# Differential attention: the two probability maps combined by ScalarE and GpSimd instead of one VectorE pass

## What is computed

```python
def _diff_scores(q, k, v, lam):
    """q (B,Q,H,2,d), k (B,K,H,2,d), v (B,K,H,2d) -> (B,Q,H,2d)."""
    s = jnp.einsum('bqhmd,bkhmd->bhmqk', q, k).astype(F32) * DIFF_SCALE
    p = jax.nn.softmax(s, axis=-1)
    attn = p[:, :, 0] - lam * p[:, :, 1]
    return jnp.einsum('bhqk,bkhe->bqhe', attn.astype(v.dtype), v)
```

## Time and profile before

| | before |
|---|---|
| median of 3 runs | 4101.81 us (4099.81 to 4107.31) |
| the profiled execution | 4105.7 us, span 4103.9 us |
| mean granted TensorE clock | 0.935 of full speed |
| PE busy | 3507.0 us (85%) |
| PE weight loads | 2879.6 us (70%) |
| DVE busy | 2514.7 us (61%) |
| ACT busy | 1064.3 us (26%) |
| POOL busy | 779.5 us (19%) |

### The profile page before, as it was taken

One profiled execution on the slowest core, in us unless ns is written; L12 is line 12 of the kernel. 1 busy time (PEld: TensorE's weight loads), 2 busy tenths in 40 slices (PEclk: granted clock), 3 DMA queues, 4 the chain that ended last, 5 costly groups with the idle time before them and its releaser, 6 DMA issues. The chain is left out here.

```text
span 4103.9 us, 51032 instructions
## 1 busy us (share of the span) xinstructions
PE 3507.0 (85%) x19424; PEld 2879.6 (70%) x19424; DVE 2514.7 (61%) x5060; ACT 1064.3 (26%) x1823; POOL 779.5 (19%) x464
## 2 busy tenths in 40 slices
PE   6798999999687775996997878999998788859888
PEld 2687888888577774775783666788886677737577
DVE  4136577753289995765554234677763799967554
ACT  2112222222144443332111211222211444413310
POOL 3233333332100001110002233433332000012000
PEclk8899999999899997998998989999999899989999
DMA  5253222232343312334325154232232633123432
GB/s 203 57 153 126 91 90 94 90 99 73 106 127 92 91 34 94 106 99 164 106 82 190 50 136 151 77 94 92 89 99 67 173 85 85 38 103 112 133 115 70
DMA packets 414142, 424.54 MB, mean 103 GB/s; under 512 B 56940, under 2 KB 350572, under 8 KB 412742
## 3 DMA queue, kind: packets, MB, share of 16 engines
q1 hardware_dynamic: 368876, 319.55, 27.0%
q10 hardware_dynamic: 45024, 101.73, 7.0%
HBM read 288.28 MB, written 124.53 MB: 101 GB/s over the span
## 5 line engine op out<-in xcount | busy, mean ns | idle before, releaser
L734 PE MATMUL l_p_acc<-l_u_hi,l_p_w_hi 128*128 128x512 f32 (+1 forms) x2240 | 612.7, 376 | 47.8 <-POOL l_p_w_lo L649 37.2
L734 PE MATMUL l_p_acc<-l_u_hi,l_p_w_lo 128*128 128x512 f32 (+1 forms) x2240 | 593.2, 367 | 0.0
L734 PE MATMUL l_p_acc<-l_u_lo,l_p_w_hi 128*128 128x512 f32 (+1 forms) x2240 | 592.3, 367 | 0.0
L734 PEld LDWEIGHTS l_p_acc<-l_u_hi,l_p_w_hi 128*128 128x128 f32 x2240 | 390.9, 190 | 126.5 <-POOL l_p_w_lo L649 37.8
L734 PEld LDWEIGHTS l_p_acc<-l_u_hi,l_p_w_lo 128*128 128x128 f32 x2240 | 386.0, 189 | 72.2
L734 PEld LDWEIGHTS l_p_acc<-l_u_lo,l_p_w_hi 128*128 128x128 f32 x2240 | 385.9, 189 | 72.2
L647 POOL TENSOR_TENSOR l_p_w_hi<-l_p_wt,l_p_zero 128x1024 fp32r<-128x1024 f32 x104 | 209.9, 2019 | 974.2 <-PE l_p_acc L734 807.7
L2014 POOL TENSOR_TENSOR l_sd_xend<-l_sd_tok,l_sd_mine 128x512 f32<-128x512 f32 x80 | 85.5, 1071 | 1285.9 <-ACT l_sd_tok L1969 1285.1
L1471 PE MATMUL l_at_pS<-l_at_k_hi,l_at_q 128*128 128x512 f32 (+1 forms) x400 | 166.3, 416 | 148.6 <-ACT l_at_prob L1586 114.0
L649 POOL TENSOR_TENSOR l_p_w_lo<-l_p_wt,l_p_w_hi 128x1024 fp32r<-128x1024 f32 x104 | 272.7, 2622 | 8.2
L1655 DVE TENSOR_REDUCE l_at_nmax<-l_at_pS 128x1 f32<-128x1280 f32 (+1 forms) x144 | 197.1, 1369 | 84.4 <-PE l_at_pS L1472 81.3
(11 more groups left out here) (329 smaller groups left out, 7067.8 us busy)
## 6 DMA issues: line engine op xcount, KB each, us to landing
l_p_wt<-w_in SPq DMA_DIRECT2D x104, 512.0 KB, 3.9
l_n_wa<-w_ada SPq DMA_DIRECT2D x10, 2048.0 KB, 18.4
xbc_d<-l_p_fin ACTq DMA_DIRECT2D x32, 640.0 KB, 2.9
kf_d<-l_p_R SPq DMA_DIRECT2D x72, 256.0 KB, 3.5
l_o_oT<-o_d SPq DMA_DIRECT2D x18, 1024.0 KB, 6.7
l_at_K<-kf_d SPq DMA_DIRECT2D x64, 256.0 KB, 2.9
l_o_rows<-w_out SPq DMA_DIRECT2D x32, 512.0 KB, 4.5
qk_d<-l_p_late ACTq DMA_DIRECT2D x12, 1280.0 KB, 4.8
```

The lines of the kernel that those rows point to most:

```text
L734: mm = pe.matmul(acc[:, a:a + w], (w_hi, w_lo)[wp][:, m % 2, k], (u_hi, u_lo)[up][:, k, t0 + c:t0 + c + w], start=(k == n == 0), stop=(k = ...
```

## The change

DVE's `combine` becomes `factor`: the reciprocal and the factor stay, the pass over the keys goes. ACT gets `scale_map(i-1)`, which multiplies the second map by the factor in place; it stands behind `copy(i-2, 1)` and ahead of `exp(i, 0)`. POOL gets a program of its own with one `tensor_tensor` add per unit, which writes `mix` and increments `mixed`. Two semaphores are new: `back_ready` (DVE to ACT) and `map_scaled` (ACT to POOL). Buffers and all other code are the same.

```diff
+                def scale_map(n):
+                    h, q = units[n]
+                    act.wait_ge(back_ready, n + 1)
+                    second = prob[:, (2 * n + 1) % 3, 0:keys(q)]
+                    act.activation(second, second, ACT.Copy, scale=back[:, n % 2:n % 2 + 1]).then_inc(map_scaled, 1)
+
...
                     if turning > 2:
                         copy(i - 2, 1)
+                    if 1 <= i < NU + 1:
+                        scale_map(i - 1)
                     if i < NU:
                         exp(i, 0)
...
+            @block.gpsimd
+            def _(pool):
+                for n, (h, q) in enumerate(units):
+                    pool.wait_ge(map_scaled, n + 1)
+                    if n >= 2:
+                        pool.wait_ge(turned, before[n - 1])
+                    w = keys(q)
+                    pool.tensor_tensor(mix[:, n % 2, 0:w], prob[:, 2 * n % 3, 0:w], prob[:, (2 * n + 1) % 3, 0:w], ALU.add).then_inc(mixed, 1)
...
-                def combine(n):
+                def factor(n):
                     h, q = units[n]
                     s = n % 2
                     dve.wait_ge(exped, 2 * n + 2)
                     dve.reciprocal(recip[:, n % 4], sums[:, s]).then_inc(mix_step, 1)
-                    dve.wait_ge(mix_step, 2 * n + 1)
-                    dve.tensor_scalar(back[:, s:s + 1], recip[:, n % 4, 1:2], sums[:, s, 0:1], lam[:, 0:1], ALU.mult, ALU.mult).then_inc(mix_step, 1)
-                    dve.wait_ge(mix_step, 2 * n + 2)
-                    if n >= 2:
-                        dve.wait_ge(turned, before[n - 1])
-                    dve.scalar_tensor_tensor(mix[:, s, 0:keys(q)], prob[:, (2 * n + 1) % 3, 0:keys(q)], back[:, s:s + 1], prob[:, 2 * n % 3, 0:keys(q)], ALU.mult, ALU.add).then_inc(mixed, 1)
+                    dve.wait_ge(mix_step, n + 1)
+                    dve.tensor_scalar(back[:, s:s + 1], recip[:, n % 4, 1:2], sums[:, s, 0:1], lam[:, 0:1], ALU.mult, ALU.mult).then_inc(back_ready, 1)
```

More of the change, by code:

```diff
@@ L1334, in attention_hyena_stage @@
     with stage(nc, tag + "lam_in", tag + "s00_in", tag + "s01_in", tag + "s10_in", tag + "s11_in", tag + "v0_in", tag + "v1_in",
-               tag + "lam_step", tag + "lam_exp", tag + "scored", tag + "maxed", tag + "exped", tag + "mix_step", tag + "mixed", tag + "turned",
+               tag + "lam_step", tag + "lam_exp", tag + "scored", tag + "maxed", tag + "exped", tag + "mix_step", tag + "back_ready", tag + "map_scaled", tag + "mixed", tag + "turned",
                tag + "turned_copied", tag + "pv_done", tag + "squared", tag + "log_done", tag + "rms_ready", tag + "scaled", tag + "o_turned",
@@ L1340, in attention_hyena_stage @@
                tag + "q_mm", tag + "q_copied", tag + "z_step", tag + "out_ready", tag + "hy_stored") as (ctx, sems):
[L1341 to L1344, removed]
+        (lam_in, s00_in, s01_in, s10_in, s11_in, v0_in, v1_in, lam_step, lam_exp, scored, maxed, exped, mix_step, back_ready, map_scaled, mixed, turned, turned_copied,
+         pv_done, squared, log_done, rms_ready, scaled, o_turned, gated, stored0, stored1) = sems[:27]
+        u_in, x_in, k_in = sems[27:31], sems[31:35], sems[35:37]
+        (kn_in, mats_in, rows_turned, rows_copied, dft_step, r_ready, x_mm, prod_step, y_ready, q_mm, q_copied, z_step, out_ready, hy_stored) = sems[37:]
         stored = (stored0, stored1)
@@ L1738, in _ @@
                     if 1 <= i < NU + 1:
-                        combine(i - 1)
+                        factor(i - 1)
                     if step_of(i) is not None:
```

## The result

The changed kernel takes **4203.1 us** (median of 4 runs, 4201.6 to 4213.5) against 4100.8 (4 runs) for the kernel before: ratio **1.0242**, 95% interval 1.0223 to 1.026, 99 us slower. The forecast was 4143, with a range of 4115 to 4188: the direction was right, the size not, and the time lies above the range. The profiled execution took 4202.85 (span 4201.1, before 4103.9), so the profile stands for the median. The mean granted TensorE clock of the whole span fell from 0.935 to 0.920.

What follows compares the result with a forecast made beforehand. DVE, busy 97 to 99% in mid-attention, was taken to set the pace. Terms -1 + 10 + 3 + 15 + 6 + 9 - 2 + 1 = +41 us on the median 4101.8 gave 4143 us; range 4115 to 4188.

Steps and rivals of the forecast that it cites:

- the delay of the exp, step by step: Attention iteration: ACT's scaling moves first exp from S+1.52 to S+3.48, second maximum to S+5.51; 0.17 of 1.47 us stays.
- The cycle forecast at 50.4: Steady attention: the four-iteration cycle takes 50.4 against 50.5 us, -1 us over some 11 cycles in both layers.
- layer 0, i = 2 to 14: Opening of layer 0's attention: DVE waits for PE without steady Hyena work, so exp shifts are paid, +6 us.
- layer 0, i = 33 to 39: Last seven of layer 0: Hyena over or thin, DVE waits for PE, every exp shift is paid, 12.6 us.
- layer 1, i = 0 to 8: Opening of layer 1's attention: long units at once, shifts of 1.65, 1.3 and 0.3 us paid, +9 us.
- all between (steady, short units, slow stretches): Other attention iterations: steady cycles -1, slow PE stretches +10 and +3, short units -2 us.
- slow PE stretches lose their cover: Attention: low-clock PE values, hidden by DVE's work before, now cost 1.2 us each in about 8 cycles, +10 us.
- its second rival: PE's low clock spreads to two positions of the cycle: 25 iterations x 1.7, +43 us, 4186; 13%.
- values of 4 us in more than one position of the cycle: Sign in PE's attention value matmuls: values of 4 us in two positions would show the forecast wrong (the clock).
- POOL asks behind the products' start: Attention: POOL's sum asks for the port at S+3.65, after the last two products start: zero, bounds -0 and +1.4 an iteration.
- The first, POOL first at the port: With scaling ended 0.3 earlier, POOL holds the port before the last two products: +1.4 in some 36 iterations, +50, 4193; 10%.
- Faster: DVE's 1.47 us is saved in each steady attention iteration because scaling doesn't delay the exp: 60 less, 4042; 5%.

Runs made afterwards that it cites:

- the kernel without POOL and with PE kept busy: Changed kernel with DVE adding the maps instead of POOL, and PE repeating the second map's last 512-column scores piece four times before the waiting piece: 4146.6 us, 1.0106.
- the kernel with POOL behind the products: Changed kernel with one more wait: POOL's sum starts only after Hyena's products of that iteration are done; 4198.3 us, ratio 1.0223.
- without POOL: Changed kernel in which ACT still scales ahead of the first exp but DVE adds the maps behind the products, POOL idle: 4189.2 us, ratio 1.0209.
- both edits: Changed kernel with POOL's sum waiting for the products and PE repeating the second map's last 512-column scores piece four times: 4145.2 us, ratio 1.0098.
- the late split: Changed kernel, scaling behind the first exp, DVE keeping its pass for 384 columns: 4143.1 us; with POOL's sum also waiting for the products, 4101.8 us.
- the late scaling: Changed kernel with ACT's scaling moved behind the first exp, in front of the last copy: 4137.5 us, ratio 1.0078.

## Why the prediction was right and wrong

**Right: the delay of the exp, step by step.** First exp at S+3.48 (forecast S+3.48), scaling 1.36 (1.37), POOL's sum 2.91 (3.0) from S+3.65, second maximum at S+5.90 to 6.01 behind the copy (5.94). The cycle forecast at 50.4 is there, at 50.36, as soon as PE stays at full clock. The terms of the other stretches can be read from starts of first maxima, in the kernel without POOL and with PE kept busy, and in the changed kernel:

| stretch | forecast | no POOL, PE kept busy | after |
|---|---|---|---|
| layer 0, i = 2 to 14 | +6 | +5.4 | +12.4 |
| layer 0, i = 33 to 39 | +12.6 | +12.3 | +14.7 |
| layer 1, i = 0 to 8 | +9 | +6.1 | +15.7 |
| all between (steady, short units, slow stretches) | +10 | +11.8 | +40.9 |

The changed kernel's column adds to 83.7. The rest of its 97 us of span lies outside these stretches: 8.0 between the last first maximum of layer 0 and the first one of layer 1, 6.8 behind the last of layer 1, less 1.3 ahead of i = 2. The forecast had 2.1 for the one end and 1 for the other; in the kernel with POOL behind the products, whose attention is nearly the same, the first of these gaps was 0.4 shorter than before, so part of it is what such stages differ by from run to run. I didn't separate it.

**Wrong: the step "slow PE stretches lose their cover", +10.** The price per stretch was 1.2 and is 1.3 to 1.7 (43 us for 32 series less, 53 for 32); the number of stretches was far off, 50 slow series where the forecast reckoned with some ten. The forecast took the one position of the earlier trace rows with a wait of 4.82 as the only one that falls to the low clock, and said itself, under its second rival, that PE now waits 2 us or more in every position; that rival had 13% and 4186. It is the case that came, and so did its sign: values of 4 us in more than one position of the cycle. Measured as a difference, PE's low clock is worth 53 us in the changed kernel (without the port: 4198.3 to 4145.2) and 43 without POOL. The step failed by one instance standing for a count: in the trace before, 11 of 13 waits of 2 us or more had slow values behind them, and none of the 41 shorter ones. With these 41 turned into long ones, that table gives some 35 more slow series; 39 came. The loop adds to it: the forecast put PE's loop at 11.9, so 1.6 us more of values are more than DVE's short iterations (11.4 to 12.2) can cover, and there a slow series is paid nearly in full (periods of 13.5 to 13.7).

**Wrong: the step "POOL asks behind the products' start", zero.** The time of asking was right to 0.01 us, but the step took the four products for one piece of work that POOL would have to stand behind. POOL began between the last two of them. The bound of +1.4 that stood beside it was close to what came (6.80 against 5.51, so +1.29), in the iterations where ACT isn't behind its copy. By the Trainium skill (SBUF — State Buffer, "Who interferes with whom") whoever issues first holds the shared ports for its whole instruction; the trace agrees, since the last product ended 0.29 behind POOL's sum, and shows the unit of that: one instruction, not a series. In time it costs little here, 1.0242 to 1.0223, since PE is late anyway; with PE kept busy 24 us, and 41 to 46 in the late split.

The sum of the two: with both edits 40 are left (1.0098), close to the forecast's 41, and with 15 slow series, not many more than the ten or so that the forecast reckoned with; the clock is 51 more (1.0223 less 1.0098), and the port 8 more (1.0242 less 1.0223), the last inside its own error. That 4145 lies so near to 4143 is partly luck: by the starts of maxima in that run the part between lost 13.8 for a term of 10, layer 0's last iterations 9.9 for 12.6 and layer 1's first 6.0 for 9.

**The rivals.** The first, POOL first at the port, named the right mechanism with a condition (the scaling 0.3 earlier) that wasn't needed. The second is the main cause. Faster would have needed a second maximum before S+4.9; the late scaling gave S+4.10 and was still slower, so that rival's own condition was not enough: it left out the second exp's wait for POOL and the butterflies that stand behind POOL's sum.

**What stays open.** Why the iteration at 1286.55 keeps the full clock after the same wait of 2.31 as its neighbours isn't settled; seven of the 54 long waits are like that. Three slow series of the changed kernel have no such wait in front of them, and their cause wasn't looked for. Four buffers for the exps, which would take the second exp's wait for POOL away, weren't tried.

## What to carry to other kernels

Before work is moved off the busiest engine, follow the queue that takes it to what stands behind it there: 1.3 us on ACT ahead of the exp cost more than the 1.5 us that left DVE. If that makes PE wait longer, count in the trace before how often a wait of the new length has slow matmuls behind it; one instance is no count. And when two causes hide each other, take them away together as well as alone: the port looked like 5 us, less than the runs can tell from nothing, and was 24.

## What the hardware showed unexpectedly

- POOL gets the port between two products that DVE runs back to back: it began 0.10 before the second, during the first, and the second took 3.13 in place of 0.42.
- A maximum, with its input in PSUM, ran at 1.49 while POOL's sum was running (1290.62 to 1293.52), and in the kernel with both edits 20 maxima lie wholly inside such a sum, each at 1.49. The Trainium skill (SBUF — State Buffer, "Who interferes with whom") says of reductions that they never contend; no row of before could show it. The maximum of the first case:

```profile
1292.45 1.49 DVE L1672 TENSOR_REDUCE l_at_nmax<-l_at_pS 128x1 f32<-128x1280 f32 x1 [1.72 <-PE l_at_pS L1472]
```

- More matmuls made the kernel faster: four repeats of a piece in PE's wait of 1.8 to 2.3 us took 33 to 53 us away, and cost nothing in the kernel before.
- POOL's f32 sum takes 2.91 in the mean for 1280 columns, 2.10 for 896 and 1.54 for 640.
